# A hybrid decoder layer on one core: x is turned before it is normalised, and three small loads move to ScalarE's queue

## What is computed

```python
def rms_norm(x, g):
    xf = x.astype(jnp.float32)
    y = xf * lax.rsqrt(jnp.mean(xf * xf, axis=-1, keepdims=True) + EPS)
    return (y * g.astype(jnp.float32)).astype(x.dtype)

h = rms_norm(x, attn_norm_g[l])
u = h @ w_in[l]            # (256, 1024) @ (1024, 3360), split by columns
...                        # two mixers (sparse attention; gated delta rule) read parts of u
...                        # output projection, residual, then top-4-of-32 experts with SwiGLU
```

## Time and profile before

| what | us |
|---|---|
| median of 3 runs | 1139.36 |
| lowest and highest run | 1138.60, 1142.78 |
| span of the profiled execution (first to last instruction) | 1135.0 |
| TensorE busy in it | 1072.2 (94%) |
| VectorE, ScalarE, GpSimd busy | 333.4, 187.3, 28.1 |
| mean granted TensorE clock | 0.991 of full speed |

### The profile page before, as it was taken

How to read it: one execution, slowest core, us unless ns; L and a number is a source line. 1 busy time by engine, 2 the same in 40 slices (tenths; PEclk the granted TensorE clock), 3 DMA queues, 4 the chain that set the end, 5 groups by cost and what they waited for, 6 DMA issues and landing times.

```text
span 1135.0 us, 12287 instructions
## 1 busy us (share of the span) xinstructions
PE 1072.2 (94%) x5057; PEld 435.3 (38%) x5057; DVE 333.4 (29%) x743; ACT 187.3 (16%) x370; POOL 28.1 (2%) x39
## 2 busy tenths in 40 slices
PE   8999979999999999999799999999998999998997
PEld 5577565433333333333233333333333333333332
DVE  2467744322221313222113222313131213222222
ACT  4257742410100000001000101000001000101000
POOL 0001410000000000000000000000000000000000
PEclk9999999999999999999899999999999999999999
DMA  9825247899999999999999999999999999999994
GB/s 328 266 82 139 60 196 277 325 423 428 431 436 431 428 432 432 427 434 431 428 430 434 429 431 432 428 432 434 427 433 432 427 434 431 430 431 432 427 421 165
DMA packets 37687, 430.58 MB, mean 379 GB/s; under 512 B 8700, under 2 KB 14364, under 8 KB 23676
## 3 DMA queue, kind: packets, MB, share of 16 engines
q1 hardware_dynamic: 37628, 429.74, 90.5%
HBM read 428.09 MB, written 1.64 MB: 379 GB/s over the span
## 4 chain that ended last, share of the span: by engine, by line
PE 75%; DMA 12%; DVE 5%; ACT 4%; issue 2%; SPq 1%; DVEq 0%; POOL 0%; ACTq 0%; POOLq 0%
PE bank L1086 52%; DMA ring<-in_exp_w_up_dram 7%; PE bank L1145 4%; DMA nsa<-in_exp_w_up_dram 3%; PE bank L646 3%; ACT nsa L1189 3%; PE bank L659 3%; PE bank L1023 3%; PE bank L1055 2%; PE bank L929 2%; PE bank L677 2%; DVE nsa L2016 1%; PE bank L1130 1%; DVE nsa L2010 1%; DMA block_rows<-ring 1%
## 5 line engine op out<-in xcount | busy, mean ns | idle before, releaser
L1086 PE MATMUL bank<-ring,nsa 128*64 128x512 f32 x2464 | 546.4, 598 | 12.8 <-ACT nsa L1189 6.6
L1086 PEld LDWEIGHTS bank<-ring,nsa 128*64 128x64 f32 x2464 | 175.3, 138 | 365.4 <-issue 347.9
L1189 ACT ACTIVATE nsa<-bank 128x512 f32<-128x512 f32 (+7 forms) x151 | 76.1, 524 | 498.3 <-PE bank L1055 236.1
L1086 PE MATMUL bank<-nsa 128*64 128x512 f32 x608 | 134.3, 594 | 3.7 <-ACT nsa L1189 1.4
L1998 DVE TENSOR_SCALAR nsa<-bank 128x512 f32<-128x512 f32 x32 | 22.1, 692 | 238.5 <-PE bank L1086 238.5
L2026 DVE COPY nsa<-bank 64x512 f32<-64x512 f32 x32 | 22.2, 693 | 208.4 <-PE bank L1086 208.4
L1186 ACT ACTIVATE nsa<-nsa 128x512 f32<-128x512 f32 (+3 forms) x36 | 21.4, 594 | 351.4 <-DVE nsa L1998 351.4
L1086 PEld LDWEIGHTS bank<-nsa 128*64 128x64 f32 x608 | 42.9, 137 | 89.9 <-issue 84.6
L1145 PE MATMUL bank<-nsa 128*128 128x512 f32 x128 | 59.5, 604 | 12.5 <-ACT nsa L1189 12.5
L2010 DVE TENSOR_SCALAR nsa<-bank 128x512 f32<-128x512 f32 (+1 forms) x33 | 22.3, 675 | 163.5 <-PE bank L1086 163.5
L1055 PE MATMUL bank<-rA,nsa 128*64 128x512 f32 x256 | 60.4, 592 | 0.1
(11 more groups left out here) (237 smaller groups left out, 577.3 us busy)
## 6 DMA issues: line engine op xcount, KB each, us to landing
ring<-in_exp_w_gate_dram SPq DMA_DIRECT2D x22, 4096.0 KB, 31.4
ring<-in_exp_w_up_dram SPq DMA_DIRECT2D x22, 4096.0 KB, 31.8
ring<-in_exp_w_down_dram SPq DMA_DIRECT2D x21, 4096.0 KB, 31.5
nsa<-in_exp_w_down_dram SPq DMA_DIRECT2D x6, 4096.0 KB, 28.0
nsa<-in_exp_w_up_dram SPq DMA_DIRECT2D x5, 4096.0 KB, 30.9
nsa<-in_exp_w_gate_dram SPq DMA_DIRECT2D x5, 4096.0 KB, 34.9
ring<-in_exp_w_down_dram SPq DMA_DIRECT2D x9, 2048.0 KB, 12.4
ring<-in_exp_w_gate_dram SPq DMA_DIRECT2D x8, 2048.0 KB, 12.4
```

What stands on the lines that cost most here:

```text
L1086: i = pe.matmul(o[64 * fh:64 * fh + 64, :], lt, wc, start=(opens and cc == 0), stop=(cc == 7), skip_group_check=True)
L1189: return nc.scalar.activation(o, i, ACT.Copy)
```

## The change

The row factor leaves the path between x and the transposes. TensorE turns x itself, as soon as it has landed; the copies times the gain go to `xTr` (where `h` was). `uc` uses `xTr`, and its result is scaled by the row factor when ScalarE copies it out. For the other projections, a new job `rb` spreads the row factors over a bank (one product of a broadcast with the identity), and VectorE multiplies `xTr` by it into `hT`. The loads of the identity, the gains and the last 8 columns of slab "c" are issued on ScalarE's queue, and on SyncE's queue slab "c" comes before tile 1 of x. `turn_x(1)` moves to between the 5th and the 6th step of `uc` 0.

```diff
 SLABS = ["c", "b", "a", "q1", "q0", "q2", "z", "w1k", "w1v", "wo_nsa", "wo_gdn"]
-PIECES = {"c": 2, "wo_nsa": 2}
+PIECES = {"wo_nsa": 2}
 QKV = [2, 3, 0, 1, 4, 5]
...
 def pe_front_order():
-    j = [("gT",)] + [("hT", 0, i) for i in range(2)] + [("uc", 0)] + [("hT", 1, i) for i in range(2)]
-    j += [("uc", 1)] + [("ub", t) for t in range(T2)] + [("vecT",)]
+    j = [("gT",)] + [("hT", 0, i) for i in range(2)] + [("rb", 0), ("uc", 0)] + [("hT", 1, i) for i in range(2)]
+    j += [("uc", 1), ("rb", 1)] + [("ub", t) for t in range(T2)] + [("vecT",)]
     j += [("ua", 0), ("gc",), ("gb", 0), ("gb", 1), ("ua", 1)] + [("qkv", QKV[0]), ("qT", 0), ("kT", 0), PROJ[0]]
     for i, (t, b, g) in enumerate(attn_steps()):
         if i == 3:
...
         ident = marks[:, C_ID:C_ID + P]
         ones = cst[:, C_ONE:C_ONE + P]
         xt = x[:, :].rearrange("p (t d) -> p t d", t=T2)
-        h = rA[:, :].rearrange("p (t d) -> p t d", t=T2)
+        xTr = rA[:, :].rearrange("p (c t) -> p c t", c=KC)
         hT = rB[:, :].rearrange("p (c t) -> p c t", c=KC)
         cin = rC[:, :].rearrange("p (m t) -> p m t", m=12)
         cv = rD[:, :].rearrange("p (m t) -> p m t", m=12)
...
                     sp.dma_start(v, wi[:, :, cols[name]:cols[name] + 512]).then_inc(landed[s], 16)
                 elif name == "c":
                     sp.dma_start(v[:, :, 0:280], wi[:, :, 1024:1304]).then_inc(landed[s], 16)
-                    sp.dma_start(v[:, :, 280:288], wi[:, :, 3352:3360]).then_inc(landed[s], 16)
                 elif name in ("w1k", "w1v"):
                     src = a["cmp_k_w1" if name == "w1k" else "cmp_v_w1"][0]
                     sp.dma_start(dst.rearrange("p (j n) -> p j n", j=16),
...
             xi = a["x"][0].rearrange("(t p) d -> t p d", p=P)
             sp.dma_start(xt[:, 0, :], xi[0]).then_inc(sem("x0_landed"), 16)
-            sp.dma_start(gv[0:KC, :], a["attn_norm_g"][0].rearrange("(c p) -> c p", p=P)).then_inc(sem("gain_landed"), 16)
-            sp.dma_start(marks[:, :], a["const_table"][:, 0:C_ONE]).then_inc(sem("ident_landed"), 16)
+            load("c")
             sp.dma_start(xt[:, 1, :], xi[1]).then_inc(sem("x1_landed"), 16)
-            load("c")
             row(B_DT, 4, "gdn_dt_bias", "decay_rows")
             row(B_AL, 4, "gdn_a_log", "decay_rows")
             load("b")
...
             done(pe.transpose(o[:, 0:KC], gv[0:KC, :], ident[0:KC, 0:KC]), ("gT",))
             def turn_x(t):
+                pe.wait_ge(sem(f"x{t}_landed"), 16)
                 for i in range(2):
-                    pe.wait_ge(sem("h1_ready" if i else "h0_ready"), t + 1)
                     o = take(("hT", t, i))
                     for c in range(4):
-                        m = pe.transpose(o[:, c * P:(c + 1) * P], h[:, t, (4 * i + c) * P:(4 * i + c + 1) * P], ident)
+                        m = pe.transpose(o[:, c * P:(c + 1) * P], xt[:, t, (4 * i + c) * P:(4 * i + c + 1) * P], ident)
                     done(m, ("hT", t, i))
+
+            def norm_row(t):
+
+                pe.wait_ge(sem("rstd_ready"), t + 1)
+                o = take(("rb", t))
+                done(pe.matmul(o[:, 0:P], bcast(ssx[:, t:t + 1], [P, P]), ident, start=True, stop=True), ("rb", t))
             def natural(job, t, name, n, between=None):
                 s, val, _ = slab[name]
                 w = ringv(s).rearrange("p (c n) -> p c n", c=KC)
                 pe.wait_ge(landed[s], val)
-                copied(pe, ("hT", t, 0)), copied(pe, ("hT", t, 1))
+                if job == "uc":
+                    pe.wait_ge(sem("ab_landed"), 16)
+                    copied(pe, ("hT", t, 0)), copied(pe, ("hT", t, 1))
+                else:
+                    copied(pe, ("rb", t))
+                turned = xTr if job == "uc" else hT
                 o = take((job, t))
                 for c in range(KC):
-                    if between and c == 4:
+                    if between and c == 5:
                         between()
-                    m = pe.matmul(o[:, 0:n], hT[:, c, t * P:(t + 1) * P], w[:, c, 0:n],
+                    m = pe.matmul(o[:, 0:n], turned[:, c, t * P:(t + 1) * P], w[:, c, 0:n],
                                   start=(c == 0), stop=(c == KC - 1))
                 done(m, (job, t))
...
                 done(m, job)
             turn_x(0)
+            norm_row(0)
             natural("uc", 0, "c", 288, between=lambda: turn_x(1))
             natural("uc", 1, "c", 288)
+            norm_row(1)
             for t in range(T2):
                 natural("ub", t, "b", 512)
             pe.wait_ge(sem("vec_landed"), 80)
...
                 evac(job, [dst], [o[:, :].rearrange("p (h d) -> p h d", h=4)])
+            act.dma_start(marks[:, :], a["const_table"][:, 0:C_ONE]).then_inc(sem("ident_landed"), 16)
+            act.dma_start(gv[0:KC, :], a["attn_norm_g"][0].rearrange("(c p) -> c p", p=P)).then_inc(sem("gain_landed"), 16)
+            act.dma_start(ringv(slab["c"][0]).rearrange("p (c n) -> p c n", c=KC)[:, :, 280:288],
+                          wi[:, :, 3352:3360]).then_inc(sem("ab_landed"), 16)
             act.wait_ge(sem("idle_ready"), 1)
             act_(vnew_[:, 511:512], vnew_[:, 510:511], ACT.Sqrt)
             def turned_x(t):
                 o = full(act, ("hT", t, 0))
                 for c in range(4):
-                    ins = nc.scalar.mul(hT[:, c, t * P:(t + 1) * P], o[:, c * P:(c + 1) * P], gT[:, c:c + 1])
+                    ins = nc.scalar.mul(xTr[:, c, t * P:(t + 1) * P], o[:, c * P:(c + 1) * P], gT[:, c:c + 1])
                 read(ins, ("hT", t, 0))
             for t in range(T2):
                 act.wait_ge(sem(f"x{t}_landed"), 16)
-                act_(h[:, t, :], xt[:, t, :], ACT.Square, accum_out=ssx[:, t:t + 1]).then_inc(sem("ssx_ready"), 1)
+                act_(rD[:, D * t:D * t + D], xt[:, t, :], ACT.Square, accum_out=ssx[:, t:t + 1]).then_inc(sem("ssx_ready"), 1)
                 root(ssx[:, t:t + 1], "msx_ready", "rms_ready", t + 1)
-                act.wait_ge(sem("rstd_ready"), t + 1)
-                nc.scalar.mul(h[:, t, 0:512], xt[:, t, 0:512], ssx[:, t:t + 1]).then_inc(sem("h0_ready"), 1)
                 copied(act, ("gT",))
                 turned_x(t)
             for t in range(T2):
+                act.wait_ge(sem("rstd_ready"), t + 1)
                 o = full(act, ("uc", t))
-                evac(("uc", t), [nrm[:, t, 10:12, :], uc[:, t, :]],
-                     [o[:, 0:128].rearrange("p (h d) -> p h d", h=2), o[:, 128:288]])
+                nc.scalar.mul(nrm[:, t, 10:12, :], o[:, 0:128].rearrange("p (h d) -> p h d", h=2), ssx[:, t:t + 1])
+                read(nc.scalar.mul(uc[:, t, :], o[:, 128:288], ssx[:, t:t + 1]), ("uc", t))
             act.wait_ge(sem("sc_ready"), 1)
             act.wait_ge(sem("decay_rows"), 32)
...
             for t in range(T2):
                 dve.wait_ge(sem("ssx_ready"), t + 1)
                 rstd(ssx[:, t:t + 1], D, "msx_ready", "rms_ready", "rstd_ready")
-                V.tensor_scalar(h[:, t, 512:1024], xt[:, t, 512:1024], ssx[:, t:t + 1], None, ALU.mult)\
-                    .then_inc(sem("h1_ready"), 1)
                 o = full(dve, ("hT", t, 1))
-                read(V.tensor_tensor(hT[:, 4:8, t * P:(t + 1) * P], h4(o[:, :]),
-                                     bcast(gT[:, 4:8].unsqueeze(2), [P, 4, P]), ALU.mult), ("hT", t, 1))
+                link_read(V.tensor_tensor(xTr[:, 4:8, t * P:(t + 1) * P], h4(o[:, :]),
+                                          bcast(gT[:, 4:8].unsqueeze(2), [P, 4, P]), ALU.mult), ("hT", t, 1))
+                copied(dve, ("hT", t, 0))
+                o = full(dve, ("rb", t))
+                read(V.tensor_tensor(hT[:, :, t * P:(t + 1) * P], xTr[:, :, t * P:(t + 1) * P],
+                                     bcast(o[:, 0:P].unsqueeze(1), [P, KC, P]), ALU.mult), ("rb", t))
             def conv(i):
```

More of the change, by code:

```diff
@@ L342, in hybrid_block @@
         cmax = stat(1)
-        h2 = h
+        h2 = rA[:, :].rearrange("p (t d) -> p t d", t=T2)
         x2T = nsa[:, 2560:4608].rearrange("p (c t) -> p c t", c=KC)
```

## The result

| kernel | median us (22 runs each) | span of the profiled execution |
|---|---|---|
| before | 1139.17 | 1135.0 |
| changed | 1141.08 | 1139.1 |

The ratio of the changed kernel to the one before is 1.0017, 95% interval 1.001 to 1.0025: slower by 1.9 us, where 1.8 us faster was forecast. That is within 0.5%, but it is clear of the scatter and has the other sign.

The account below looks back on a forecast made before the run. The expert weight stream sets the pace and starts when TensorE's gapless front frees slots, so time gained before 14 us reaches the end. -1.57 - 0.49 + 0.25 = -1.8 us took 1139.36 to 1137.6; range 1135.5 to 1141.5.

Parts of the forecast that it names:

- part 2: Order of the loads before `uc` 0: slab "c" lands at 8.9 to 9.4, `uc` 0 starts at 9.25 instead of 10.82.
- the sum: Start of `ub`: -1.57 for `uc` 0, -0.49 for tile 1's stall, +0.25 for the `rb` product, together -1.8 us.
- part 3: Added work: `rb` 1 costs TensorE 0.25 us; `rb` 0, VectorE's two products, ScalarE's factors and its issues (in part 2) cost nothing.
- no stall at tile 1: TensorE before tile 1's transposes: the 0.49 us wait for scaled x disappears, if tile 1 lands at about 10.6.
- no later than the 10.82 of now: Latest bound on the start of `uc` 0: the 10.82 us of the kernel before; sum's worst bound -0.3 us.
- The first rival: Small piece on ScalarE's queue served last: lands at 10.76, `uc` 0 at 10.82, sum -0.24, time 1139.1; chance 0.13.
- the part that I had added for scatter: Widening of the range for run scatter: from the cases' 1137.4 to 1140.0 out to 1135.5 to 1141.5.
- four cases: Forecast 1137.6 (0.75), small piece last 1139.1 (0.13), gain absorbed 1139.4 (0.07), tile 1 of x late 1140.0 (0.05).

Follow-up runs that it names:

- e5: Kernel before with the norm's part of the change alone, all loads on SyncE in the old order; median 1139.94 us, ratio 0.9999 to the kernel before.
- e6: Kernel before with slab "c" and the 32 KB piece ahead of tile 1 on SyncE, identity and gains on ScalarE's queue; median 1138.37 us, ratio 0.9989.
- e1: Changed kernel with the 32 KB piece (last 8 columns of slab "c") back on SyncE's queue behind slab "c"; median 1136.70 us, ratio 0.998 to before.
- e11: Kernel before with spare products filling TensorE's waits at 64 us (3) and 143 us (5), nothing else; median 1140.11 us, ratio 1.0002.
- e12: Kernel before with identity, gains and the 32 KB piece on ScalarE's queue, norm and SyncE's order unchanged; median 1139.16 us, ratio 1.0001.
- e4: Changed kernel with SyncE waiting for the 32 KB piece to land before it issues slab "b"; one run, 1139.0 us.
- e3: Changed kernel with 9 more zero products on TensorE before `uc` 0 to keep it busy; median 1141.69 us, ratio 1.0027 to the kernel before.
- e7: Changed kernel run once more without any edit, to look at the clock; 1139.3 us.
- e2: Changed kernel with the 32 KB piece issued first on ScalarE's queue, ahead of identity and gains; median 1136.54 us, ratio 0.9979 to the kernel before.
- e8: Repeat of e1 without any further edit, to look at the clock; 1136.1 us.
- e9: e1 plus 3 spare products on TensorE in its wait at 64 us; median 1135.24 us, ratio 0.9971 to the kernel before.
- e10: e9 plus 5 spare products on TensorE in its wait at 143 us; median 1137.54 us, ratio 0.9982 to the kernel before.

## Why the prediction was wrong

**What held.** The transposes started at 7.42 (7.1 forecast; the zero products before them ended later). Slab "c" landed at 8.2 and tile 1 at 1.67 + 7.9 = 9.6, both sooner than the 8.9 and 10.6 of part 2. The `rb` product, VectorE's two products (1.22 us each for the 1.4 of the sum) and ScalarE's issues were hidden where part 3 put them, and there is no stall at tile 1. That both parts must be done sooner for `uc` 0 to start sooner is what e5 and e6 show (alone, the norm's part was worth nothing and the loads' part about 1.2 us, by medians); with the piece on SyncE's queue the marker moved by 2.0 us and the time by 2.3 (e1), for a forecast of 1.8.

**The step that failed is in part 2**: "no later than the 10.82 of now". I took the landing of before as the latest bound for the piece, because the bytes in front of it were the same or fewer. It is no bound even for a load that keeps its place: with SyncE's loads as they were, the piece landed at 10.76 in the profile of before, 11.46 in e5 and 11.86 in e11. On ScalarE's queue the piece had only 100 KB ahead of it; it had neighbours instead. From 6 to 8.5 us each of its packets (64 per DMA engine) passed against one of SyncE's, and those grew from 1.1 KB (slab "c", e12) to 2 KB on average (the last of slab "c", and tile 1) just because slab "c" had been moved ahead. By 9.0 us 671 of ScalarE's packets had passed instead of e12's 955. The next microsecond passed only 182 more with the DMA engines more than half idle (e4), and why is open; the last ones stood beside slab "b". It landed at 12.45, and at 12.7 and 12.6 in e3 and e7.

**The first rival** had the right place and the wrong price: "lands at 10.76 as now", 1139.1. I had put the rule of the Trainium skill (DMA: Bandwidth & Descriptors, section Queues, rings and completion order: the engines take turns between queues, a packet at a time) on the side that speaks against this rival. The trace agrees with the rule in these stretches, 185 packets to 185 and 298 to 300; the page's packet is some 9 to 17 descriptors, and whether the profile's packets of 32 bytes are the same thing no run shows. My inference from the rule was the mistake: turns that are equal in number give a queue of 32-byte packets next to nothing in bytes, for as long as the other one has work. The same page's section Issuing engines are not separate DMA queues says that another issuing engine saves the issue time only. Here the landing went with it, 12.45 or 8.4 (e1), as the other queue also means another place in line and other neighbours; first on ScalarE's own queue the load landed at 4.95 (e2). The measurement decides.

**A term was missing**: what the clock makes of a wait. The sum priced an idle TensorE at its own length. The wait of 3.6 us in the first profile was followed by 1.7 us of lost clock; that of 3.1 us in the second (e7) by none. With the piece late, the marker is 1.67 or 3.15 us late; the measured 1.9 us lie between. That they are a mean over runs with and without the fall is argued from two profiles, not shown. Against e11's marker the two are 1.05 and 2.53 us late.

**What the sum left alone.** The 4.36 us between median and span are no fixed part of the time: in every run with both numbers it is about 1.8. They came from comparing a median with the span of one execution that was near the lowest (1136.8 by that estimate).

**The chances.** That the change would be within 0.5% was right. The range held the median of 1141.08 only through the part that I had added for scatter, which is luck: none of its four cases reached it.

**Open.** Why the piece, issued at 1.82, sent hardly a packet before about 5.5 us, while slab "c", issued at 1.22, had been moving since about 4; in e2, issued ahead of the slab, it was through by then. What holds it back was not tried. What slows both queues from 8.5 to 10 us, while slab "b" is issued and hardly moving. Why e3 gained nothing at the end.

## What to carry to other kernels

In the busy stretches of this trace two DMA queues shared the engines by turns of one packet, not by bytes (185 to 185, at 2 KB and 32 bytes). A load of many tiny packets that something waits for did well behind its neighbours on their queue (8.4) or first on its own (4.95), and badly behind others beside a stream of large packets (12.45). The landing of a load before a change is no upper bound after it: here it moved by 1.1 us with nothing changed, and by more once the load had other neighbours. And when two things bound one instruction, ask for each part of a change what it is worth alone; here one was worth nothing alone and the other, by the medians, about half of what both brought together (1.2 us of 2.3, with intervals that overlap).

## What was unexpected of the hardware

The products on zeros that open the kernel end at different times from run to run: the gains' turn behind them started between 6.73 us (e1) and 7.94 us (e7) in kernels whose TensorE does the same up to there, and at 6.73, 6.76, 6.90 and 7.62 in e1, e8, e9 and e10, which are one kernel up to there. That moves the whole front by as much unless a DMA ends later. And an idle stretch of the same length, 1.7 us near 66 us, was followed by a granted clock of 0.77 to 0.80 in e1 and e8 and of 1.00 in e4 and in the kernel before, whose row is:

```profile
64.00:68.00 4.00, 2.30 (x17) 1.67 (x17) 3.79 (x12) 1.34 (x5) 0.00 (x0) 1.00 0.36 90
68.00:72.00 4.00, 4.00 (x21) 3.56 (x20) 3.79 (x15) 2.23 (x9) 0.00 (x0) 1.00 1.09 364
```

So two single profiles of one kernel can differ by 1.5 us at the marker (36.89 and 35.41 for the changed one) for reasons that no edit has; only the ratios over many runs could be trusted below that.
